# In-projection stage of a two-layer hybrid trunk: norm sums and spreads placed inside later tiles, query and key products ahead of the values

## The reference, cut to what matters

```python
h = rms_norm(x, mix_norm_g[l])
u = h @ w_in[l]
c_q, c_kv, k_rope, z, xs, bs, cs, dt_raw, xr, gate = split_cols(u, IN_SPLITS)
# attention: q = rms_norm(c_q) @ w_uq, rotated in its last 32 columns;
#            k, v = rms_norm(c_kv) @ w_ukv;  k_rope rotated and shared by the 8 heads
# state space: silu(conv(xs, bs, cs)), dt = softplus(dt_raw + bias), gate z
# recurrence: xr = conv(xr); r, i = sigmoid(block_diag(xr)); a = exp(-8 r softplus(-lam))
#             u = sqrt(-expm1(2 log a)) * i * xr; h = scan(a, u); y = rms_norm(h * gelu(gate))
```

## Time and profile before

| | |
|---|---|
| median of 3 runs | 3324.66 us (3321.38 to 3326.13) |
| profiled execution: span, first to last instruction | 3324.6 us |
| time of a run beyond its span | under 0.1 us by these two numbers |
| PE products busy | 3055.6 us, 92% |
| DVE busy | 1213.0 us, 36% |
| ACT busy | 702.7 us, 21% |
| POOL busy | 1147.0 us, 35% |
| mean granted TensorE clock | 0.964 of 2.4 GHz |

### The profile page before, as it was taken

The page is one execution under the profiler, slowest core; times in us unless marked ns, Lnnn a source line. Parts: engine busy times, 40 slices in busy tenths (PEclk is TensorE's granted clock), DMA queues, the critical chain, the costliest instruction groups (busy, mean ns, idle before and its releaser), DMA issues. The chain is left out here.

```text
span 3324.6 us, 35224 instructions
## 1 busy us (share of the span) xinstructions
PE 3055.6 (92%) x14184; PEld 2403.5 (72%) x14184; DVE 1213.0 (36%) x1195; ACT 702.7 (21%) x1143; POOL 1147.0 (35%) x598
## 2 busy tenths in 40 slices
PE   4888899989999999999978889999999999999996
PEld 3765557877778888888767645688768788888885
DVE  6365446303432222222254644452044222222223
ACT  3034553103211010010121355521031111111011
POOL 2221123473234343343232122235703334334341
PEclk9889999999999999999988899999999999999998
DMA  3000001121011111111010000012201111111111
GB/s 133 32 23 12 5 1 58 51 89 45 28 42 45 50 49 46 50 44 50 27 57 32 18 9 1 14 57 70 89 13 44 38 51 45 49 50 44 50 48 59
DMA packets 41937, 142.99 MB, mean 43 GB/s; under 512 B 7024, under 2 KB 9072, under 8 KB 41200
## 3 DMA queue, kind: packets, MB, share of 16 engines
q1 hardware_dynamic: 41840, 141.67, 12.6%
HBM read 135.89 MB, written 5.77 MB: 43 GB/s over the span
## 5 line engine op out<-in xcount | busy, mean ns | idle before, releaser
L491 POOL TENSOR_TENSOR wsp<-raw,ones 128x1024 fp32r<-128x1024 f32 x236 | 455.5, 1930 | 1624.4 <-PE ps L610 1470.6
L610 PE MATMUL ps<-hB,wsp 128*128 128x512 f32 x3840 | 876.3, 390 | 5.4 <-DVE hB L1501 3.3
L610 PEld LDWEIGHTS ps<-hB,wsp 128*128 128x128 f32 x3840 | 721.3, 188 | 156.6 <-ACT hB L1168 4.1
L610 PE MATMUL ps<-hm,wsp 128*128 128x512 f32 x3072 | 703.5, 390 | 0.0
L610 PEld LDWEIGHTS ps<-hm,wsp 128*128 128x128 f32 x3072 | 575.3, 188 | 125.6 <-DVE x L1594 6.1
L494 POOL TENSOR_TENSOR wsp<-raw,wsp 128x1024 fp32r<-128x1024 f32 x236 | 576.5, 2443 | 18.5
L610 PE MATMUL ps<-hA,wsp 128*128 128x512 f32 x2112 | 495.6, 397 | 54.0 <-POOL wsp L494 38.3
L610 PEld LDWEIGHTS ps<-hA,wsp 128*128 128x128 f32 x2112 | 404.2, 192 | 144.0 <-POOL wsp L494 39.0
L1594 DVE TENSOR_TENSOR x<-ps,x 128x1024 f32<-128x1024 f32 x128 | 156.8, 1225 | 474.7 <-PE ps L610 472.5
L1231 ACT ACTIVATE ss<-ss 128x1024 f32<-128x1024 f32 x32 | 34.0, 1061 | 896.3 <-DVE ss L1576 896.3
L885 PE MATMUL ps<-hA,wsp 128*128 128x512 f32 x768 | 177.3, 390 | 10.2 <-POOL wsp L491 10.2
(11 more groups left out here) (261 smaller groups left out, 2681.6 us busy)
## 6 DMA issues: line engine op xcount, KB each, us to landing
raw<-in_weight_tiles SPq DMA_DIRECT2D x236, 512.0 KB, 3.3
x<-in_xT SPq DMA_DIRECT2D x1, 4096.0 KB, 14.9
outT<-x SPq DMA_DIRECT2D x8, 512.0 KB, 3.1
wh<-in_head_weights SPq DMA_DIRECT2D x8, 256.0 KB, 2.8
mem_s<-memory_normed SPq DMA_DIRECT2D x2, 1024.0 KB, 4.8
memp<-in_memT SPq DMA_DIRECT2D x1, 1024.0 KB, 4.9
memory_normed<-memp SPq DMA_DIRECT2D x1, 1024.0 KB, 4.1
pos_i<-in_positions SPq DMA_DIRECT2D x1, 512.0 KB, 5.7
```

The source lines that it names most:

```text
L491: pool.tensor_tensor(wsp[:, s, 0, :], raw[:, s, :], ones[:, 0:1].to_broadcast([P, TILE]), ALU.mult).then_inc(w_ready[s], 1)
L610: last = pe.matmul(ps[:, 2 * buf + half, 0:n], w[:, k, col:col + P], rhs(part, k, half * n, n), start=(at_k == 0 and w is w_hi and part == 0),
```

## The change

PE, DVE, ACT, POOL and SP get a new order within the input projection. In words, and then the core of the diff:

- `stats` is cut in two: `sum_cols` (the one-column sums) and `spread`. `halves` runs a tile with something between its chunks 0 to 3 and 4 to 7; `whole` runs one tile.
- Input norm: sums after the first pair, the spread inside the c_kv tile, which goes to banks 4 and 5; the spread goes to banks 6 and 7. DVE takes the two c_q tiles after it.
- c_q and c_kv: both sums after the first gate tile (into banks 7 and 6), both spreads inside the second gate tile (the c_kv norm has columns of its own, in `root3` and `rcol3`).
- Recurrence's norm: sums after the second xs tile, the spread inside the b tile; DVE makes the reciprocal after the first xs convolution and scales after the second.
- The squares of x alternate between `sq` and `rs`.
- Recurrence: with r' = tanh(..) and a, DVE computes (a*a + 1)*r' in two instructions in place of r'/(r' + 1) in three, and ACT's root has no factor 2.
- Rotation: SP loads the table ahead of the third weight tile, in four transfers; DVE rotates the key into `ss` right after the mixed tile; ACT copies it to the first pair of heads, DVE to the second.
- After the last tile: keys and queries first (banks 4 to 7, 0, 1), then the values (bank (b+2) mod 8). ACT's activation of c comes after the query copies. The first scores wait for the values, the key copies and the first head's `rope_add`, the second scores for the second head's.
- POOL does `rope_add` of heads 0 and 1 before it waits for `prep` and `act_done`.

```diff
 SP
+                    sp.wait_ge(pst, 32)
+                    for half in range(2):
+                        sp.dma_start(cs[half][NOPE:DQ, :], rope_d[0:ROPE, tokens]).then_inc(ld_rope, 16)
+                        sp.dma_start(cs[half][DQ:P, :], rope_d[DQ:P, tokens]).then_inc(ld_rope, 16)
                     with sp.Fori(1, R_OUT) as i:
                         load_pair(i, 2 * i)
...
-                    sp.wait_ge(conv_done, 6)
-                    sp.wait_ge(gate_done, 4)
-                    sp.wait_ge(pst, 32)
-                    sp.dma_start(cs[NOPE:DQ, :], rope_d[0:ROPE, :]).then_inc(ld_rope, 16)
-                    sp.dma_start(cs[DQ:P, :], rope_d[DQ:P, :]).then_inc(ld_rope, 16)
 POOL
-                    pool.wait_ge(prep, 2)
-                    pool.wait_ge(act_done, 8)
                     rope_add(0)
                     rope_add(1)
+                    pool.wait_ge(prep, 1)
+                    pool.wait_ge(k_rope, 4)
+                    pool.wait_ge(act_done, 8)
 PE
+                    def halves(n, buf, between, free=None):
+                        s, u = n % 2, n // 2
+                        pe.wait_ge(w_ready[s], u * 2 + 2)
+                        if buf < 2:
+                            pe.wait_ge(t_free[s], u + 1)
+                        tile3(s, buf, of(hA), part_of=slice(0, 4))
+                        between()
+                        tile3(s, buf, of(hA), part_of=slice(4, 8)).then_inc(t_ready[s], 1)
...
                     pair(0, U_IN, of(hA), hooks=chunk_ready)
-                    stats(N_MIX, ss)
-                    with pe.Fori(1, 3) as i:
-                        pair(i, i, of(hA))
-                    stats(N_CQ, sq)
-                    stats(N_CKV, lr[:, 1, :])
-                    pair(3, 3, of(hA))
+                    sum_cols(N_MIX, ss)
+                    halves(T_CKV, 2, lambda: spread(N_MIX, bank=6))
+                    whole(T_MISC)
+                    whole(T_XR)
+                    whole(T_XR + 1)
+                    whole(T_GT)
+                    pe.wait_ge(bc_done, N_MIX + 1)
+                    sum_cols(N_CQ, sq)
+                    sum_cols(N_CKV, lr[:, 1, :], bank=6)
+                    def spread_ranks():
+                        spread(N_CQ)
+                        spread(N_CKV, bank=6, cols=rcol3)
+                    pe.wait_ge(t_free[0], T_CKV // 2 + 2)
+                    halves(T_GT + 1, 1, spread_ranks)
                     lru_gates(0)
-                    pair(4, 4, of(hA))
+                    whole(T_Z)
+                    whole(T_Z + 1)
                     lru_gates(1)
-                    pair(5, 5, of(hA))
+                    whole(T_XS)
+                    whole(T_XS + 1)
                     pe.wait_ge(gate_done, 4)
...
-                    stats(N_LRU, sq)
-                    pair(6, 6, of(hA))
-                    pe.wait_ge(prep, 1)
+                    sum_cols(N_LRU, sq)
+                    halves(T_B, 0, lambda: spread(N_LRU))
+                    whole(T_C)
...
+                    pe.wait_ge(bc_done, N_LRU + 1)
                     pe.wait_ge(ld_wh[0], 32)
                     for n in range(6):
-                        pe.wait_ge(v_done, n + 1)
                         if n < 2:
+                            project_k(0, n, 4 + n).then_inc(ip_ps, 1)
+                            continue
+                        if n == 2:
+                            pe.wait_ge(sp_v, 3)
+                        elif n == 4:
+                            pe.wait_ge(t_free[0], U_OUT + 1)
+                        project_q((n - 2) // 2, n % 2, (4 + n) % 8).then_inc(ip_ps, 1)
+                    pe.wait_ge(ld_wv, 16)
+                    pe.wait_ge(t_free[1], U_OUT + 1)
+                    for b in range(NBLK):
+                        if b >= 2:
+                            pe.wait_ge(ip_a, (2, 4, 5, 6, 7, 8)[b - 2])
+                        if b >= 4:
+                            pe.wait_ge(ip_v, b - 3)
+                        pe.matmul(ps[:, (b + 2) % 8, :], ckv_s[:, b * P:(b + 1) * P], wv_s[:, :],
+                                  start=True, stop=True).then_inc(v_ps, 1)
 ACT
                     for k in range(DC):
-                        if k >= 1:
-                            act.wait_ge(sq_used, k)
-                        act.activation(sq[:, :], x[:, k, :], ACT.Square).then_inc(sq_ready, 1)
+                        if k >= 2:
+                            act.wait_ge(sq_used, k - 1)
+                        act.activation((sq, rs)[k % 2][:, :], x[:, k, :], ACT.Square).then_inc(sq_ready, 1)
 DVE
-                        link(dve.tensor_scalar(d_, r_, 1.0, None, ALU.add))
-                        link(dve.reciprocal(d_, d_))
-                        link(dve.tensor_tensor(d_, d_, r_, ALU.mult))
+                        link(dve.tensor_tensor(d_, a_, a_, ALU.mult))
+                        link(dve.scalar_tensor_tensor(d_, d_, 1.0, r_, ALU.add, ALU.mult))
```

More of the change, by code:

```diff
@@ L1315, in _ @@
                     take(T_MISC, ss[:, :])
+                    dve.wait_ge(ld_rope, 64)
+                    for half in range(2):
+                        tokens = slice(half * HT, (half + 1) * HT)
+                        dve.tensor_tensor(ss[NOPE:DQ, tokens], ss[NOPE:DQ, tokens], cs[half][NOPE:DQ, :], ALU.mult)
+                        link(dve.tensor_tensor(q_tmp[NOPE:DQ, tokens], ss[DQ:P, tokens], cs[half][DQ:P, :], ALU.mult))
+                    for half in range(2):
+                        dve.tensor_scalar(cs[half][NOPE:P, :], cs[half][NOPE:P, :], SCALE, None, ALU.mult)
+                    link(dve.tensor_tensor(ss[NOPE:DQ, :], ss[NOPE:DQ, :], q_tmp[NOPE:DQ, :], ALU.add))
+                    dve.sem_inc(k_rot, 1)
                     for ch in range(2):
@@ L1318, in _ @@
                         dve.sem_inc(lru_xr, 1)
+                    take(T_GT, gt_s[:, 0, :])
                     rcol_of(N_CQ)
+                    rcol_of(N_CKV, out=rcol3[:, 0:NBLK], of=root3[:, 0:NBLK])
                     dve.wait_ge(bc_ready, N_CQ + 1)
@@ new lines, in _ @@
+                    ssm_conv(0)
+                    dve.wait_ge(dt_ps, 1)
+                    v, e, l = (sq[:, 32 * j:32 * j + 32] for j in range(3))
+                    v3 = v.rearrange("p (b h) -> p b h", h=SH)
+                    rcol_of(N_LRU)
+                    link(dve.tensor_tensor(v3, ps[:, 6, 0:256].rearrange("p (b c) -> p b c", c=32)[:, :, 0:SH],
+                                           g("dt_b", 0, SH).unsqueeze(1).to_broadcast([P, NBLK, SH]), ALU.add))
+                    dve.sem_inc(sp_v, 1)
@@ new lines, in _ @@
+                    ssm_conv(1)
+                    softplus_v(1, dtt[:, :, :].rearrange("p b h -> p (b h)"), v, e, l)
+                    link(dve.tensor_tensor(att[:, :, :], dtt[:, :, :],
+                                           aneg[:, :].unsqueeze(1).to_broadcast([P, NBLK, SH]), ALU.mult))
+                    link(dve.memset(state[:, :, :], 0.0))
+                    dve.wait_ge(bc_ready, N_LRU + 1)
+                    for ch in range(2):
+                        last = dve.scalar_tensor_tensor(gt_s[:, ch, :], gt_s[:, ch, :], g("lru_g", ch), banks(4), ALU.mult, ALU.mult)
@@ L1388, in _ @@
+                    last.then_inc(bc_done, 1)
                     dve.sem_inc(prep, 1)
[L1389 removed]
+                    ssm_conv(2)
+                    ssm_conv(3)
                     def rotate_q(head, half, bank, done):
```

154 lines of the change are left out of this document (65 added, 89 removed).

## The result

The changed kernel takes 3221.79 us (median of 4 runs, 3220.68 to 3229.41) beside 3325.39 us for the kernel before (median of 4, 3321.38 to 3330.14): a ratio of 0.9692, 95% interval 0.9678 to 0.9706. The forecast was 3222.0 us with a range of 3206 to 3240. The profiled execution is the slowest of the four, 3229.41 us with a span of 3227.7, so a run is its span and 1.7 us. By that rule the span of 3324.6 that the prediction read belongs to a run of about 3326.3 us and not to the median, so the agreement to 0.1 us that it counted on was chance; the sum of gains, 102.6 us, doesn't depend on it.

The account below looks back on a forecast made before the run. PE, busy 92% of the span, was taken to bound the kernel, losing time to waits and low clock before the first scores. 50.3 us net per layer plus 1 us each at attention gave 102.6: 3324.6 to 3222.0 us, range 3206 to 3240.

Parts of the forecast that it names:

- waits removed: Eight PE waits between the first projection product and the first scores go: 45.1 us in layer 1, 42.8 in layer 2.
- spreads at double clock: The four spreads, 14.7 us per layer at the low clock, take half at double the clock: 7.3 us less.
- wait for the first sum: Input norm: PE's wait left after double-buffering the squares, 2.8 us in layer 1, 0.5 in layer 2, bounds 0 and 5.
- reciprocal of the recurrence: Recurrence's norm: reciprocal queued on DVE behind the first xs convolution keeps 1 us of PE wait, bounds 0 to 4.
- recurrence before its sum: The 8.4 us wait before the third sum goes through a shorter DVE chain; 0 left, upper bound 2.4 us.
- tail, key copies behind POOL's add: Before the first scores: DVE's two key copies, possibly held by POOL's add, leave 1.8 us of wait, range 1.2 to 2.6.
- falls of the clock: Sums themselves bring PE's clock down: two drops per layer of 2 us each, 4 us, bounds 0 and 8.
- start of attention: Query products at the first scores run at full clock without idleness ahead: 1 us gained per layer, bounds 0 and 2.
- the first rival: Sums leave no gap, so PE's clock stays up in the stage: 8 us less, 3211 us; chance 0.13.
- DVE as the bound: DVE's chains in the stage, meeting POOL's splits, keep more PE waits: 17.5 us more, 3240 us; chance 0.14.
- The low clock through the tiles: After sums between tile halves the clock stays low, 11 us more per tile; with six tiles 3354 us; chance 0.02.
- That the change did nothing: Some late condition in the stage keeps PE as long as the old bubbles did: 3325 us; chance 0.01.

Follow-up runs that it names:

- the rank sums apart: Changed kernel with the c_q and c_kv sums one tile apart instead of back to back; 3216.32 us, ratio 0.9675 to the kernel before.
- later key copies: Changed kernel with DVE's two key copies for the second pair of heads moved behind the first row maximum; 3217.17 us, ratio 0.9682.
- the best version: Changed kernel with each sum cut into groups among tile chunks, and DVE's two key copies behind the first row maximum; 3211.96 us, ratio 0.9646.
- the kernel with the reciprocal: Changed kernel with the recurrence's three instructions, including the 6.55 us reciprocal, back in place of two; 3245.18 us, ratio 0.9763.

## Why the prediction was right, and where it was not

The total came out within 1 us of the forecast, closer than the kernel repeats itself (3215.5 to 3229.4 us over eight runs), so the last few us of the agreement are luck. By its own steps, with the stage first: predicted 203 and 201 us, measured 205.0 and 198.4 in the first trace and 197.3 and 198.4 in the second.

| step, us per layer | predicted | measured, layer 1 / layer 2 |
|---|---|---|
| waits removed | 45.1 / 42.8 | all of them gone from the list |
| spreads at double clock | 7.3 | 7.1 |
| wait for the first sum | 2.8 / 0.5 | 3.2 and 0 in two traces / 0 |
| reciprocal of the recurrence | 1 | 0 or 1.1, the latter only where the clock stayed up |
| recurrence before its sum | 0, bound 2.4 | 0 |
| tail, key copies behind POOL's add | 1.8 | 2.3 |
| falls of the clock | 4 | 6.6 and 0 in two traces / 3.2 |
| start of attention | 1 gained | 0 / 0, and 0.6 in layer 1 of the second trace |

**Sums and spreads inside tiles.** Right in its mechanism and sizes. With the cover taken away, both PE's waits (11.6 us) and the low clock of the spreads return.

**Squares.** Right: two buffers take ACT out of the chain. The adds meet POOL's splits as foreseen, three of the eight in layer 1 take longer than 1.23 us. DVE's timeline of the changed kernel:

```profile
50.13 2.80 DVE L1318 TENSOR_TENSOR ss<-ss,sq 128x1024 f32<-128x1024 f32 x1
52.96 3.31 DVE L1318 TENSOR_TENSOR ss<-ss,rs 128x1024 f32<-128x1024 f32 x1
...
60.09 2.80 DVE L1318 TENSOR_TENSOR ss<-ss,rs 128x1024 f32<-128x1024 f32 x1
```

What is left of the wait is between 0 and 3.3 us, by where the splits fall.

**Recurrence.** Right, both reasons: 6.1 us of chain and 2.2 us from DVE being free earlier. It holds without slack: DVE ends the chain at 194.06 + 1.23 = 195.29, and the sum starts at 195.40.

**Clock.** A short row of sums can bring it down with PE never idle, and this decided between the forecast and the first rival. The step was mis-sized in two ways. A fall costs 1.6 us of half tile, not 2 (3.4 us where a wait stands ahead of it, in the first sum of layer 1: 1.0 on the sum, 2.4 on the half tile). And the third one is not a cost beside the reciprocal's 1 us but in its place, which the prediction added. It named three places and counted two falls; there were three in layer 1 of the first trace, two in layer 2, and in the second trace none and two. The 2.8 us for the b and c pair was read from one trace, too: against 22.12 us that pair took 24.88 there, but 23.53 in layer 2 of the same trace and 23.36 and 23.66 in the second trace of the kernel before, so 1.2 to 1.5 us is its usual size.

The Trainium skill, in "TensorE: Matmul & The Clock Gate", section "Why this matters for your kernels", asks for no idle gaps between bursts of matmuls. The windows of 130 to 134 us show a fall with no gap at all, and with the rank sums apart the same products bring none, so on this kernel the rule is not enough; by it the double sum would have cost nothing, and it cost 1.6 us in 13 of 14 layers.

**Tail.** Named rightly: 2.3 us in place of the old 1.4 and 7.5, with the cause in DVE's two copies behind POOL's add. Its size was 0.5 us short, inside the bounds of 1.2 to 2.6; the add held the copies for 2.1 us (3.43 against 1.29). The Trainium skill, in "SBUF — State Buffer", section "Who interferes with whom", lists copies, too, among what can take VectorE's shared port and so exclude a GpSimd instruction; the two rows agree.

**Start of attention.** This step failed. The four query products behind the first scores took 3.60 us in the first trace, as long as the 3.48 of the earlier trace rows, so the clock is low there as before. The step took the low clock to go with the wait of 7.5 us, while the tail's own term left 1.8 us of it; 2.3 us were left, and that is mostly enough: behind that wait these products were slow in 11 of 14 layers (2.9 to 3.6 us). With the later key copies, where the same products stand ahead and the wait is 0.7 us, they ran at the full clock in all four layers of the two kernels, as here:

```profile
235.00 1.93 PE L718 MATMUL ps<-cq_s,wh 128*128 128x512 f32 x4
```

And it wouldn't have mattered for the whole: the best version's attention in layer 1 was still 249.3 us behind such a start. Over both layers attention took 6.3 us more than before in the first trace and 2.7 in the second, at a lower mean clock. The kernel with later key copies shows 241.9 us in a layer, so the change doesn't bind it to be longer. Over all traces here it is 247.1 us on average in 22 layers with the change or most of it (241.9 to 249.8) and 246.0 in 6 layers without it (243.8 to 248.0); whether the change costs it a microsecond stays open. What sets the clock's path through attention isn't settled either: no run changed more of attention than the place of two key copies.

**So the 102.6 us came right partly by compensation.** Over the two traces of the changed kernel the stages gained 101.5 and 109.2 us, 105.4 on average, where I had 100.6; attention lost 4.5 on average where I had a gain of 2. Both misses are inside the range and no larger than the scatter of single traces, but they hid each other.

**The rivals.** The clock staying up is what layer 1 of the second trace shows, for one layer. (Its price was given as 8 us less and its time as 3211 us; 3222 - 8 is 3214, and the spreads "a little shorter" had no number for the other 3.) DVE as the bound would have needed a stage of 210 us; it falls. The low clock through the tiles falls with the window of 132 us, 0.97 within one half tile. That the change did nothing falls with the time and with the list of waits.

## What to carry to other kernels

Put a short row of one-column products alone between dense tiles rather than two rows in a chain (1.6 us here), and keep the product that needs its result half a tile away, so that ACT's and DVE's small steps have cover. Before removing a wait of PE, ask what the instruction behind it had been hiding: here a sum hid a buffer's release, and a slow half tile hid a reciprocal. A wait costs more than its length (8.4 us of waiting cost 10 to 12 us), since the products behind it start at the low clock, so look at the durations of the two groups behind each wait when you price it.

## What was not expected of the hardware

**The same instructions, one time with the clock and one time without.** The third sum stands behind 0.68 us of 32-column transposes and is 1.95 us long. In 14 layers of seven traces with this sequence and no wait ahead of it, the half tile behind it ran at the full clock in four (5.7 us) and not in ten (7.1 us or more). A single sum of 1.84 us between dense tiles, with no wait ahead of it, did not bring the clock down in any of these traces, and a double one of 3.7 us nearly always.

**A scan is held by GpSimd as an add is.** DVE's scan of 128x1024 took 3.87 us in the changed kernel, beside POOL's split, and 2.29 us in the kernel with the reciprocal, where it fell between splits (both rows stand with that run). The instruction of POOL that it met in the changed kernel:

```profile
186.04 4.25 POOL L494 TENSOR_TENSOR wsp<-raw,wsp 128x1024 fp32r<-128x1024 f32 x1
```

This half of POOL's split takes 2.39 us where it meets nothing. The shorter chain lost nothing by meeting the split with its scan: it was held for 1.6 us there and 2.0 us on the product behind it, and the longer chain for 1.7 and 1.9 us on two products of its own (2.93 and 3.12 us in place of 1.23). Each chain meets one split and is held by it for some 3.6 us in all, whichever instructions it falls on.
